# Latent attention: the reciprocal of the sums of p on GpSimd, and the rotation of queries in four VectorE instructions

## What is computed

```python
mod = silu(c) @ ada_w[i] + ada_b[i]            # six vectors of 2048 for each layer
x2 = x.reshape(..., ROPE // 2, 2)              # rotary part of queries and keys
x0, x1 = x2[..., 0], x2[..., 1]
x0 * cos - x1 * sin, x0 * sin + x1 * cos
s = (q_nope @ k_nope.T + q_pe @ k_pe.T) * scale
p = softmax(where(mask, s, -inf))              # exp(s - max) / sum
o = p @ v                                      # each head; then o @ w_o
```

## Time and profile before

| | |
|---|---|
| time, median of 3 runs | 2198.61 us (2198.19 to 2198.71) |
| profiled execution | 2197.71 us, span 2196.0 us |
| granted TensorE clock, mean | 0.997 |
| TensorE busy | 2139.7 us (97%) |
| VectorE busy | 1595.8 us (73%) |
| ScalarE busy | 985.2 us (45%) |
| GpSimd busy | 105.1 us (5%), 208 instructions |
| latent attention, ticks 0 to 18 | about 143 to 293 us of the span |

### The profile page before, as it was taken

The page is one execution under the profiler, slowest core; times in us unless marked ns, Lnnn a source line. Parts: engine busy times, 40 slices in busy tenths (PEclk is TensorE's granted clock), DMA queues, the critical chain, the costliest instruction groups (busy, mean ns, idle before and its releaser), DMA issues.

```text
span 2196.0 us, 24789 instructions
## 1 busy us (share of the span) xinstructions
PE 2139.7 (97%) x9557; PEld 1744.1 (79%) x9557; DVE 1595.8 (73%) x1793; ACT 985.2 (45%) x1274; POOL 105.1 (5%) x208
## 2 busy tenths in 40 slices
PE   5799999999999999999999999999999999999999
PEld 2378887888888888888778888878888888888887
DVE  6789999787777777778877666878775555455566
ACT  1076635444443444443544455564444433444443
POOL 2101100000000000000000000000000000000000
PEclk9999999999999999999999999999999999999999
DMA  9999897889998889999588778958987666666673
GB/s 387 418 353 358 351 390 280 279 298 323 350 340 320 329 313 343 324 348 355 201 285 316 268 270 283 341 177 285 342 287 230 232 195 188 217 212 212 221 237 125
DMA packets 177064, 635.90 MB, mean 290 GB/s; under 512 B 20385, under 2 KB 51377, under 8 KB 150705
## 3 DMA queue, kind: packets, MB, share of 16 engines
q1 hardware_dynamic: 147298, 427.93, 56.1%
q0 software_dynamic: 27792, 201.34, 24.5%
q10 hardware_dynamic: 1856, 5.04, 0.6%
HBM read 616.37 MB, written 17.86 MB: 289 GB/s over the span
## 4 chain that ended last, share of the span: by engine, by line
PE 85%; DVE 7%; DMA 6%; ACT 1%; issue 1%; POOL 0%; SPq 0%; ACTq 0%; DVEq 0%; POOLq 0%
PE ps L1840 53%; PE ps L1846 26%; PE ps L1857 3%; DMA gate<-in_ada_w 3%; DVE wlo L1146 2%; DVE ada_w L1183 1%; DMA ada_head<-in_ada_w 1%; DMA raw<-in_mla_w_o 1%; DVE gate L1183 1%; DVE ada_wide L1183 1%; DMA ada_w<-in_ada_w 1%; DMA raw<-in_mla_w_uv 1%; PE ps L2069 0%; DVE ada_head L1183 0%; PE ps L2099 0%
## 5 line engine op out<-in xcount | busy, mean ns | idle before, releaser
L1146 DVE TENSOR_TENSOR wlo<-raw,whi 128x1024 fp32r<-128x1024 f32 (+1 forms) x717 | 866.9, 1216 | 516.4 <-ACT whi L706 515.5
L706 ACT ACTIVATE whi<-raw 128x1024 fp32r<-128x1024 f32 (+1 forms) x717 | 756.3, 1056 | 1055.5 <-PE ps L1846 964.4
L1840 PE MATMUL ps<-whi,hT_hi 128*128 128x512 f32 x1880 | 585.7, 393 | 0.6 <-DVE hT_lo L1573 0.6
L1840 PE MATMUL ps<-whi,hT_lo 128*128 128x512 f32 x1880 | 579.6, 389 | 0.0
L1846 PE MATMUL ps<-wlo,hT_hi 128*128 128x512 f32 x1880 | 502.7, 389 | 0.0
L1840 PEld LDWEIGHTS ps<-whi,hT_lo 128*128 128x128 f32 x1880 | 352.8, 188 | 74.1
L1846 PEld LDWEIGHTS ps<-wlo,hT_hi 128*128 128x128 f32 x1880 | 352.9, 188 | 73.7
L1840 PEld LDWEIGHTS ps<-whi,hT_hi 128*128 128x128 f32 x1880 | 350.2, 188 | 71.8 <-DVE hT_lo L1573 1.1
L1183 DVE CUSTOM_DVE_ANT_0 ada_w<-ada_w,c_bc,cols 128x2048 f32<-128x2048 f32 x145 | 339.8, 2345 | 18.8 <-ACT c_bc L1031 10.3
L1840 PE MATMUL ps<-whi,uT_lo 128*128 128x512 f32 x656 | 202.0, 389 | 0.0
L1840 PE MATMUL ps<-whi,uT_hi 128*128 128x512 f32 x656 | 201.9, 389 | 0.0
(11 more groups left out here) (271 smaller groups left out, 1461.5 us busy)
## 6 DMA issues: line engine op xcount, KB each, us to landing
raw<-in_ffn_w SPq DMA_DIRECT2D x528, 512.0 KB, 4.9
ada_w<-in_ada_w POOLq DMA_DIRECT2D x145, 1024.0 KB, 8.1
raw<-in_fox_w_in SPq DMA_DIRECT2D x96, 512.0 KB, 5.2
ada_head<-in_ada_w POOLq DMA_DIRECT2D x16, 1024.0 KB, 20.3
raw<-in_mla_w_o SPq DMA_DIRECT2D x32, 512.0 KB, 8.2
raw<-in_fox_w_o SPq DMA_DIRECT2D x32, 512.0 KB, 5.6
gate<-in_ada_w POOLq DMA_DIRECT2D x12, 1024.0 KB, 8.8
ada_low<-in_ada_w POOLq DMA_DIRECT2D x10, 1024.0 KB, 10.9
```

The lines of the kernel that those rows point to most:

```text
L706: nc.scalar.activation(split_hi(pl.unit)[:, 0:n], raw[:, s, 0:n], ACT.Copy).then_inc(hi_ready, 1)
L1146: nc.vector.tensor_tensor(split_lo(pl.unit)[:, 0:n], raw[:, s, 0:n], split_hi(pl.unit)[:, 0:n].bitcast(F32), ALU.subtract).then_inc(lo_rea ...
L1840: nc.tensor.matmul(ps[:, 2 * pair + t, 0:width], a[:, t * P:(t + 1) * P], w_hi, start=(first and c == 0 and a is hi), stop=False)
```

## The change

In the latent layer the reciprocal leaves VectorE. GpSimd makes it in four operations on 128x2, each behind a semaphore of the one before: a guess by pow(sum, -1), and one Newton step, guess x (2 - sum x guess). So that it doesn't wait behind loads that can't be issued yet, GpSimd's ada loads are interleaved: before head m's reciprocal come all loads whose slot is free once the sums of tick m+1 are done (its second sum included), later ones come after it. In the forgetting layer the reciprocal stays on VectorE.

The rotation of a group's queries takes four instructions in place of six: `cos` and `sin` are held four times instead of twice, side by side, so that one multiplication covers both halves (512 elements for each partition instead of 256); the subtraction and the addition stay. ScalarE fills the two further copies at the start with four more instructions. One more memset is made at the start, and three tiles of [128, 2] are added.

```diff
+def two_sums(i):
+    return i < TICKS - 1 and i not in (0, 2, 4)
+def sums_by_tick(i):
+    return ADA_HEAD + 1 + sum(1 + two_sums(j) for j in range(i + 1))
...
+            nc.gpsimd.memset(minus_one[:, :], -1.0).then_inc(consts, 1)
...
-            for n in range(7, len(ADA_ORDER)):
+            n = 7
+            for m in range(H):
+                while ada_slot_free(n) <= sums_by_tick(m + 1):
+                    load_ada(n)
+                    n += 1
+                pool.wait_ge(exp_done, m + 1)
+                total, guess = psums[:, m % 2, :], pinv_guess[:, :]
+                nc.gpsimd.tensor_tensor(guess, total, minus_one[:, :], ALU.pow).then_inc(pinv_step, 1)
+                pool.wait_ge(pinv_step, 3 * m + 1)
+                nc.gpsimd.tensor_tensor(pinv_rest[:, :], total, guess, ALU.mult).then_inc(pinv_step, 1)
+                pool.wait_ge(pinv_step, 3 * m + 2)
+                nc.gpsimd.tensor_scalar(pinv_rest[:, :], pinv_rest[:, :], -1.0, 2.0, ALU.mult, ALU.add
+                                        ).then_inc(pinv_step, 1)
+                pool.wait_ge(pinv_step, 3 * m + 3)
+                nc.gpsimd.tensor_tensor(pinv[:, m % 2, :], guess, pinv_rest[:, :], ALU.mult
+                                        ).then_inc(inv_ready, 1)
+            while n < len(ADA_ORDER):
                 load_ada(n)
+                n += 1
...
-            for twin in range(2):
+            for twin in range(4):
...
-                t0, t1, t2, t3 = rope(x0, x1, cs, sn, *parts)
-                mark(nc.vector.tensor_tensor(x0, t0, t1, ALU.subtract))
-                nc.vector.tensor_tensor(x1, t2, t3, ALU.add).then_inc(q_roped, 1)
+                mark(nc.vector.tensor_tensor(by_cos, both, cs, ALU.mult))
+                mark(nc.vector.tensor_tensor(by_sin, both, sn, ALU.mult))
+                own()
+                mark(nc.vector.tensor_tensor(both[:, :, :, 0:ROPE], by_cos[:, :, :, 0:ROPE],
+                                             by_sin[:, :, :, ROPE:2 * ROPE], ALU.subtract))
+                nc.vector.tensor_tensor(both[:, :, :, ROPE:2 * ROPE], by_sin[:, :, :, 0:ROPE],
+                                        by_cos[:, :, :, ROPE:2 * ROPE], ALU.add).then_inc(q_roped, 1)
...
-                    if 1 <= i <= H:
+                    if 1 <= i <= H and layer == 1:
                         m = g - 1
                         dve.wait_ge(exp_done, m + 1)
                         nc.vector.reciprocal(pinv[:, m % 2, :], psums[:, m % 2, :]).then_inc(inv_ready, 1)
```

More of the change, by code:

```diff
@@ L218, in trunk @@
     kpe = place_at("kpe", [P, T, 2, P], F32, b0 + 44 * KB)
-    cos = place_at("cos", [P, T, 2, RH], F32, b0 + 46 * KB)
-    sin = place_at("sin", [P, T, 2, RH], F32, b0 + 46 * KB + KB // 2)
+    cos = place_at("cos", [P, T, 4, RH], F32, b0 + 46 * KB)
+    sin = place_at("sin", [P, T, 4, RH], F32, b0 + 47 * KB)
     mla_k = place_at("mla_k", [P, 2, T, NB], F32, b0 + 28 * KB)
@@ L298, in trunk @@
     pinv = new("pinv", [P, 2, 2])
+    minus_one = new("minus_one", [P, 2])
+    pinv_guess = new("pinv_guess", [P, 2])
+    pinv_rest = new("pinv_rest", [P, 2])
     gate_turn = new("gate_turn", [KC, P])
@@ L419, in trunk @@
         inv_ready = sem("inv_ready")
+        pinv_step = sem("pinv_step")
         p_scaled = sem("p_scaled")
@@ L444, in trunk @@
         n_small = 3
-        n_consts = 5 + 2 + 4
+        n_consts = 6 + 2 + 4
         narrow = PROJ[0] + 4 * PAIRS + 3 * D_FF // P * 4 // UC + PAIRS
@@ L659, in _ @@
             nc.gpsimd.memset(kpe[:, :, :, :], 0.0).then_inc(consts, 1)
-            pool.wait_ge(consts, 5)
+            nc.gpsimd.memset(minus_one[:, :], -1.0).then_inc(consts, 1)
+            pool.wait_ge(consts, 6)
             nc.gpsimd.affine_select(out=ident[:, :], in_=ident[:, :], compare_op=ALU.not_equal,
@@ L1521, in rope_queries @@
                 q2 = mla_q[:, g % 2, :, :].rearrange("p t (b e) -> p t b e", b=2)
-                x0, x1 = (q2[:, :, :, 2 * DH + n * ROPE:2 * DH + (n + 1) * ROPE] for n in range(2))
+                both = q2[:, :, :, 2 * DH:2 * DH + 2 * ROPE]
                 cs, sn = (x[:, :, :, :].rearrange("p t h f -> p t (h f)").unsqueeze(2).to_broadcast(
-                    [P, T, 2, ROPE]) for x in (cos, sin))
-                parts = [rope_t[:, n, :].rearrange("p (t b f) -> p t b f", t=T, b=2) for n in range(4)]
-                t0, t1, t2, t3 = rope(x0, x1, cs, sn, *parts)
-                mark(nc.vector.tensor_tensor(x0, t0, t1, ALU.subtract))
-                nc.vector.tensor_tensor(x1, t2, t3, ALU.add).then_inc(q_roped, 1)
+                    [P, T, 2, 2 * ROPE]) for x in (cos, sin))
+                by_cos, by_sin = (rope_t[:, 2 * n:2 * n + 2, :].rearrange("p a n -> p (a n)").rearrange(
+                    "p (t b f) -> p t b f", t=T, b=2) for n in range(2))
+                mark(nc.vector.tensor_tensor(by_cos, both, cs, ALU.mult))
[5 more added lines that the diff above has]
+                                        by_cos[:, :, :, ROPE:2 * ROPE], ALU.add).then_inc(q_roped, 1)
                 dve.wait_ge(q_roped, g + 2)
@@ L1591, in attention @@
                         ins.then_inc(masked, 1)
-                    if layer == 0 and i < TICKS - 1 and i not in (0, 2, 4) or layer == 1 and one_ada(i) and pl.ada < ada_end(1, SH_F):
+                    if layer == 0 and two_sums(i) or layer == 1 and one_ada(i) and pl.ada < ada_end(1, SH_F):
                         ada()
```

## The result

The changed kernel is slower: 2232.45 us, median of 4 runs (2232.11 to 2232.90), against 2198.40 for the kernel before on the same chip (its three runs of above and a fourth); a ratio of 1.0154, 95% interval 1.0142 to 1.0166, or 34 us. The time lies in the predicted range and at its upper end. It isn't the forecast's (2205.5, with its own range of 2201 to 2210) but that of the rival in which VectorE holds GpSimd up (2233). The profiled execution has a span of 2230.8 us, 34.8 above that of before.

The account below looks back on a forecast made before the run. VectorE's pace through latent attention, 145 to 293 us, was taken to bound the kernel; 5.6 + 2.0 - 0.7 = +6.9 us gave a median of 2205.5, range 2196 to 2235, likeliest case 2201 to 2210.

Parts of the forecast that it names:

- the rival in which VectorE holds GpSimd up: GpSimd reads in latent attention wait out VectorE instructions with two SBUF inputs: loop 11.1 us, time 2233; chance 0.25.
- Where the kernel is bound: Latent attention, 140 to 293 us: VectorE never rests, and the end of head 15's hT_lo carries to the kernel's end.
- The loop: Latent attention tick: reciprocal, scaling p, whi, wlo, next sum close a loop of 2.46 + 2.24 + 3.97 = 8.67 us.
- E: The moment in a latent attention tick when its second ada sum ends and wlo starts; 213.32 in tick 8.
- What GpSimd must do now: After the ada loads in each tick, four chained GpSimd operations take 1.5 us (1.16 to 1.88), reciprocal at E+2.41.
- The forecast's 8.67 for a tick: The closed loop's length in latent attention (8.33 to 9.05), against 8.06 us as run.
- The sign that it named: In the trace after, GpSimd's operations starting only where a sum or wlo ends would show the held-up rival right.
- The rival's own sum: Held-up rival, chance 0.25: 7 x 3.0 + 5 x 2.8 = 35, less 0.7, gives 2233.
- Tick 4: In latent attention, VectorE idles there for TensorE, which hides the delay: 0 us.
- The ticks with a rotation: Ticks 2, 6, 10: GpSimd's reciprocal comes at about the same time, each keeps 0.08 + 0.14 us: -0.7 in all.
- Rotation and start: Four groups' wider multiplications save 0.6 us; extra sines, cosines and memset at the start cost nothing.
- The rival "gains nothing": In the rotation, wider strided reads cost what two instructions' overhead saves: 0.6 us, inside every case; no chance of its own.

Follow-up runs that it names:

- the kernel with plain sums: The changed kernel with VectorE's sums in the latent attention's ticks replaced by plain row sums with one SBUF input: 2207.22 us, ratio 1.0041.
- the memsets: The changed kernel with GpSimd's four operations replaced by chains of 8, 4 or 22 dependent memsets that read nothing: 2201.92, 2198.16 and 2231.83 us.
- the kernel with 22 memsets: The changed kernel with GpSimd's four operations replaced by a chain of 22 dependent memsets, p scaled by a constant: 2231.83 us, ratio 1.0155.

## Why the prediction was right, and where it was wrong

**Where the kernel is bound** held: VectorE's pace through the attention, and the last hT_lo carried to the end, to within 1.3 us in all eleven kernels (a trace is one execution, the median is of several).

**The loop** held too, as a mechanism and in its terms: 2.24 from scaling p to whi and 3.97 from the wlo to the next E are both in the tick after.

**"What GpSimd must do now" is the step that failed.** It priced the four operations as if GpSimd ran alone (1.5 us, 1.16 to 1.88). In the kernel with plain sums they take 1.70 (218.32 to 220.02), and even there pow starts beneath a wlo; where nothing holds them they take 1.54 (245.94 to 247.48 in that kernel). The value taken was right for operations that run alone, but its parts weren't, and that they made up for each other is luck: pow is 0.70 at its shortest, far above the 0.29 allowed for one operation, and the others 0.19, with 0.09 between them where 0.24 was taken. The forecast's 8.67 for a tick and 2205.5 for the kernel answer to the plain sums' 8.82 and 2207.22. In the changed kernel they took 3.50 (230.21 to 233.71), as one of them sat under a sum. The text had the mechanism, as its rival, and gave it 0.25, since no row of before showed it. The range holds the measured time only through that rival; the likeliest case's own range ends at 2210, 22 us short. The sign that it named (operations that start only where a sum or wlo ends) is not quite what the trace shows: a held operation stands there as started and is long, and ends 0.13 us behind VectorE's instruction. What the rows of before did show was that VectorE is hardly ever idle and that sum and wlo have two inputs in SBUF; with the interference taken as given, the rival's 2233 followed from rows 4, 5 and 8.

**The rival's own sum** was 2233, and 2232.45 came. It put the signal at E+4.85, measured E+4.42: two free steps take 0.55 us, not 1.1. It put seven ticks at 3.0 and five at 2.8; from hT_lo to hT_lo the step behind a tick's reciprocal grew by 2.6 to 2.9 (ticks 7, 8, 9 and 11), 3.4 (tick 5), 1.7 (tick 3) and 2.2 to 2.5 (12 to 16); tick 1 cost 3.5, counted on the wlo behind it. What these fall short of 3.0 and 2.8 came from ticks that the sum had left out: tick 4, and tick 2, whose third operation was held for 2.29 us (170.14) and which cost 2.3. That the whole came out within 1 us is in part luck.

**Tick 4** was said to cost nothing, since VectorE idles there for TensorE. It cost 2.6. VectorE did idle 1.16 us there, ahead of hT_lo, but GpSimd had started only at 188.69, behind the exponent, and its third operation, with one input, fell into the next sum all the same (timeline of the changed kernel):

```profile
189.29 0.42 DVE L1612 TENSOR_TENSOR hT_lo<-ps,hT_hi 128x256 fp32r<-128x256 f32 x1 [1.16 <-ACT hT_hi L955]
...
189.63 2.34 DVE L1217 CUSTOM_DVE_ANT_0 ada_wide<-ada_wide,c_bc,cols 128x2048 f32<-128x2048 f32 x1
...
189.77 2.25 POOL L701 TENSOR_SCALAR pinv_rest<-pinv_rest 128x2 f32<-128x2 f32 x1
```

**The ticks with a rotation** (6 and 10) came out as said: their reciprocal costs nothing (the step from hT_lo to hT_lo behind them is 0.2 and 0.05 shorter than before), for the rotation gives GpSimd some 2 us more before ScalarE needs it. The operations are held there as well, by each of the rotation's instructions in turn (0.51 and 0.52 for the last two of tick 10). Tick 2, the third with a rotation, was also said to keep its saving and did not: its third operation came too late for the rotation and met the sum behind it.

**Rotation and start**: priced at 0.6 us of gain and nothing; neither can be told from zero. The rival "gains nothing" and the forecast can't be told apart in the time; in the trace the multiplications stand as forecast.

**The rule that was weighed.** Operations of 0.19 us that last 1.83 to 2.29 beside a sum with two SBUF inputs, that end 0.13 us behind it, and that take 0.20 beside one with a single input, are what the Trainium skill (SBUF — State Buffer, Who interferes with whom) states: the two engines share a read interface, and whoever comes later waits for the whole of the other's instruction. It also says that a GpSimd instruction that only writes isn't affected, which the memsets confirm, and that a sum of the `tensor_reduce` kind never contends, which the plain sums confirm. That the shared part is a port is the page's account; the runs show who waits for whom. And they show it in one direction only: in the changed kernel 12 sums start while an operation of GpSimd is running, as at 230.76 with pow until 231.08, and last 2.34 or 2.35 us like the others, without a later start. Whether VectorE ever waits for such a small operation isn't shown.

## What to carry to other kernels

Before moving small work to GpSimd, list what VectorE runs at that time and how many inputs each instruction has in SBUF: a GpSimd operation that reads waits out one with two, so each operation in a dependent chain is a fresh draw, and a chain is worth moving only if all of it fits between such instructions. Price the moved step by the moment at which its result is needed, here between 1.5 and 2.1 us after E, and not by the engine time that it frees. A small free time on the busiest engine (16 x 0.08 us) is a poor trade for a longer dependence that closes through three engines.

## What the runs showed that I had not expected

A GpSimd operation with one SBUF input is held just as one with two is: 2.25 us for the `TENSOR_SCALAR` above, 0.19 alone. pow on 128x2 takes 0.70 us at the least, more than three times a product of the same size. A chain of dependent memsets on GpSimd moves at 0.153 us each.

TensorE's granted clock fell in the longer attention. Before, it was 1.00 in each 20 us stretch from 140 to 340. After, two stretches of 10 us of the changed kernel (as in the earlier trace rows; busy PE, PEld, DVE, ACT, POOL, then the clock):

```profile
170.00:180.00 10.00, 6.17 (x34) 5.02 (x32) 7.57 (x12) 5.63 (x13) 4.27 (x6) 1.00 0.65 247
180.00:190.00 10.00, 9.81 (x52) 9.35 (x53) 5.93 (x11) 6.02 (x14) 4.42 (x8) 0.83 0.86 297
```

TensorE was busy 6.17 of 10 us, and in the next 10 the clock was 0.83 in the mean, so for part of them the lower level of 1.2 GHz instead of 2.4. Five more of the stretches up to 330 are at 0.83, and the kernel with 22 memsets has four such (180 to 190, 260 to 270, 280 to 290 and 310 to 320); the one with plain sums has none. In the ticks TensorE waits for the loop in any case; what the dips cost beyond that wasn't measured. That the idle time brings the dips about is my reading of the order in which they come, and no run was made to show it; nor does every stretch fit, for after 280 to 290 of the changed kernel, with TensorE busy 6.71 of 10 us, the clock stays at 1.00. They aren't the cause of the loss: the loop of 10.69 us is made up in full by the terms of GpSimd, ScalarE and VectorE.
